# A mixture-of-experts stage of a fused fp32 kernel on one Trainium2 core: units of 32 and of 64 rows by turns in place of units of 64, experts in index order, and the bias rows sent behind the sixth weight piece

## What is computed

```python
def moe_ffn(h, w_router, b_router, w_gate_up, b_gate_up, w_down, b_down):   # h: 512 x 1024
    logits = tok @ w_router + b_router                   # 32 experts
    top_logit, top_idx = lax.top_k(logits, TOP_K)        # TOP_K = 4
    top_w = jax.nn.softmax(top_logit, axis=-1)
    ...
    def expert_block(args):
        xe, e = args
        gu = xe @ w_gate_up[e] + b_gate_up[e]            # 1024 -> 2048
        gate = jnp.minimum(gu[:, :D_FF], SWIGLU_LIMIT)
        up = jnp.clip(gu[:, D_FF:], -SWIGLU_LIMIT, SWIGLU_LIMIT)
        act = (up + 1.0) * gate * jax.nn.sigmoid(SWIGLU_ALPHA * gate)
        return act @ w_down[e] + b_down[e]               # 1024 -> 1024
    ...                                                  # sum over a token's 4 experts, weighted by top_w
```

## Time and profile before

| | |
|---|---|
| median of 3 runs | 3230.87 us (3229.05 to 3233.18) |
| profiled execution, its own time | 3228.85 us |
| its span, first to last instruction | 3227.0 us |
| TensorE busy | 3110.0 us, 96% |
| mean granted clock of TensorE | 0.989 of 2.4 GHz |
| first matmul of the expert loop | 1096.51 us |
| last transposes of the expert stage | 2249.12 us |

### The profile page before, as it was taken

One profiled execution on the slowest core, in us unless ns is written; L12 is line 12 of the kernel. 1 busy time (PEld: TensorE's weight loads), 2 busy tenths in 40 slices (PEclk: granted clock), 3 DMA queues, 4 the chain that ended last, 5 costly groups with the idle time before them and its releaser, 6 DMA issues.

```text
span 3227.0 us, 40980 instructions
## 1 busy us (share of the span) xinstructions
PE 3110.0 (96%) x14106; PEld 1840.9 (57%) x14107; DVE 1303.3 (40%) x2108; ACT 841.3 (26%) x1605; POOL 357.4 (11%) x328
## 2 busy tenths in 40 slices
PE   7999999889999999999999999999999999999999
PEld 5555556464787633333333333333787888888887
DVE  2465564624445312121212121212567577454552
ACT  3354453610211211111111111111325355211100
POOL 0112021431000000000000000000301344000000
PEclk9999999989999899999999999999999999999999
DMA  5324233326312699999999997897411121222121
GB/s 217 118 79 137 91 111 124 121 118 217 122 53 106 233 350 391 374 385 388 389 391 388 379 391 283 310 364 272 155 77 71 59 84 38 94 87 81 63 79 56
DMA packets 190022, 632.85 MB, mean 196 GB/s; under 512 B 18752, under 2 KB 56000, under 8 KB 179168
## 3 DMA queue, kind: packets, MB, share of 16 engines
q1 hardware_dynamic: 161216, 552.79, 44.9%
q0 software_dynamic: 10944, 39.85, 3.5%
q10 hardware_dynamic: 17760, 38.78, 3.4%
HBM read 594.78 MB, written 36.57 MB: 196 GB/s over the span
## 4 chain that ended last, share of the span: by engine, by line
PE 84%; DMA 5%; DVE 4%; issue 2%; ACT 2%; SPq 1%; POOL 1%; ACTq 0%; DVEq 0%; POOLq 0%
PE ps L322 24%; PE ps L2338 17%; PE ps L2312 11%; PE ps L2024 9%; PE ps L271 6%; DMA slot<-in_w_exp 5%; PE ps L2076 2%; PE ps L2567 2%; PE ps L2085 2%; PE ps L1954 1%; PE ps L2539 1%; PE ps L2307 1%; PE ps L2522 1%; PE ps L2303 1%; SPq L1364 1%
## 5 line engine op out<-in xcount | busy, mean ns | idle before, releaser
L2338 PE MATMUL ps<-slot,xT_blk 128*64 128x512 f32 x3200 | 733.9, 599 | 28.2 <-DMA slot<-in_w_exp 25.9
L2338 PEld LDWEIGHTS ps<-slot,xT_blk 128*64 128x64 f32 x3200 | 218.2, 137 | 464.8 <-issue 376.1
L2312 PE MATMUL ps<-slot,aT 128*64 128x512 f32 x1632 | 362.6, 597 | 0.9 <-ACT aT L1715 0.9
L2024 PE MATMUL ps<-hT,slot 128*128 128x512 f32 (+1 forms) x896 | 307.6, 501 | 0.8 <-DVE sum_row L2669 0.8
L2312 PEld LDWEIGHTS ps<-slot,aT 128*64 128x64 f32 x1632 | 117.1, 137 | 238.1 <-issue 238.1
L3063 DVE TENSOR_TENSOR gate<-ps,b_row 128x512 f32<-128x512 f32 x50 | 34.6, 692 | 517.5 <-PE ps L2338 517.2
L2024 PEld LDWEIGHTS ps<-hT,slot 128*128 128x128 f32 x896 | 168.0, 190 | 129.1 <-issue 120.2
L2697 DVE SCALAR_TENSOR_TENSOR conv<-ps,g_conv,conv 128x510 f32<-128x510 f32 (+1 forms) x224 | 133.3, 631 | 179.7 <-ACT conv L1505 176.3
L3059 DVE MEMSET b_there<- 128x1 f32 x50 | 3.0, 59 | 386.7 <-DMA b_few<-in_b_gu 379.3
L1690 ACT ACTIVATE y_row<-ps 128x512 f32<-128x512 f32 x51 | 30.5, 597 | 383.5 <-PE ps L2312 383.5
L322 PE MATMUL ps<-in_t,in_s 128*128 128x264 f32 x528 | 124.7, 386 | 0.5 <-issue 0.5
(11 more groups left out here) (510 smaller groups left out, 4717.7 us busy)
## 6 DMA issues: line engine op xcount, KB each, us to landing
slot<-in_w_exp SPq DMA_DIRECT2D x768, 512.0 KB, 8.5
in_w<-in_w_ffn SPq DMA_DIRECT2D x22, 1024.0 KB, 4.8
expert_rows<-zero SPq DMA_DIRECT2D x4, 4608.0 KB, 22.1
slot<-in_w_xbc SPq DMA_DIRECT2D x8, 2048.0 KB, 7.6
sum_here<-sum_rows ACTq DMA_DIRECT2D x32, 512.0 KB, 3.7
w_modT<-in_w_modT POOLq DMA_DIRECT2D x32, 512.0 KB, 3.8
rnn_w<-in_w_rnn SPq DMA_DIRECT2D x16, 1024.0 KB, 4.8
expert_rows<-y_row ACTq DMA_DIRECT2D x102, 128.0 KB, 5.6
```

What stands on the lines that cost most here:

```text
L2024: last = pe.matmul(ps[:, 2 * (m % 2) + part, 0:n], w[:, (k * 4 + m % 4) * P:(k * 4 + m % 4 + 1) * P], hT[:, k, c0:c0 + n], start=(k == 0), ...
L2312: last = pe.matmul(ps[h * UNIT:(h + 1) * UNIT, 6, :], aT[:, t, d * UNIT:(d + 1) * UNIT], slot[4 + d][:, t * D + h * 512:t * D + (h + 1) * ...
L2338: last = pe.matmul(ps[h * UNIT:(h + 1) * UNIT, 2 * s + t, :], xT_blk[:, k, s * UNIT:(s + 1) * UNIT], slot[i // 4][:, at:at + 512], start=( ...
```

## The change

Turns are kept, but the two units of a turn now have 32 rows (s = 0) and 64 rows (s = 1), and a turn gathers 96 rows. The experts stand in index order. An expert begins where the one before it ended, with either size, and takes units by turns until its tokens have room. With the counts above that makes 60 units in 30 turns. Experts 0, 4, 21, 23 and 30 get a single unit of 32 rows; 1, 11, 22 and 31 a single one of 64; nineteen get one of each (96 rows); expert 9 gets 128 rows, 7 and 24 get 160, and 20 gets 192.

A 32-row matmul takes 32 partitions of output. The two pieces of one K tile are laid out as four quarters of gate and up columns, and the four matmuls go to four column tiles. Down of a 32-row unit is four matmuls of 256 columns for each piece. Gate and up of a unit now come out of the same piece, so the first step on VectorE waits for gu15. `turn_act` moves from behind gu4 to behind gu5, the down pieces from behind gu5 to behind gu7. Buffers that were shared by the two units of a turn (`aT`, `y_row`, `b_row`, `b_few`, the PSUM banks of both) are now one for each size. Every expert gets bias rows for both sizes, eight DMAs in place of four, issued behind piece gu5 in place of gu15. The places come from a scan over the parity of each expert's units.

```diff
-UNIT = 64
-UNITS = SEQ * TOPK // UNIT + NE - 1
+UNIT_ROWS = [32, 64]
+UNIT_AT = [0, 32]
+PERIOD = 96
+TILES = [P // n for n in UNIT_ROWS]
+PART = D // TILES[0]
+PERIODS = -(-(SEQ * TOPK + NE * (UNIT_ROWS[1] - 1)) // PERIOD)
+UNITS = 2 * PERIODS
...
-    TURN_AT, DOWN_AT = 5, 6
+    TURN_AT, DOWN_AT = 6, 8
...
-        for h in range(2):
-            act.dma_start(expert_rows[bass.ds(u * UNIT, UNIT), h * 512:(h + 1) * 512], y_row[h * UNIT:(h + 1) * UNIT, :]).then_inc(s_yrow, 16)
+        rows, first = UNIT_ROWS[s], i * PERIOD + (UNIT_ROWS[1] if s == 0 else 0)
+        width = D // TILES[s]
+        for j in range(TILES[s]):
+            act.dma_start(expert_rows[bass.ds(first, rows), j * width:(j + 1) * width],
+                          y_row[s][j * rows:(j + 1) * rows].rearrange("p t c -> p (t c)")).then_inc(s_yrow[s], 16)
...
-        with sp.Fori(1, NE) as q:
-            u = sp.value_load(first_unit[0:1, bass.ds(q, 1)], min_val=1, max_val=UNITS)
-            e = sp.value_load(expert_at[0:1, bass.ds(q, 1)], min_val=1, max_val=NE - 1)
+        with sp.Fori(1, NE) as e:
+            u = sp.value_load(first_unit[0:1, bass.ds(e, 1)], min_val=1, max_val=UNITS)
             for i in range(GU_PIECES):
                 sp.wait_ge(moe_pe.sem, moe_pe.before(f"gu{i}", u))
                 load_piece(i, e)
-            sp.wait_ge(moe_dve.sem, moe_dve.before("spread", u))
-            load_bias(e)
+                if i == 5:
+                    sp.wait_ge(moe_dve.sem, moe_dve.before("spread", u))
+                    load_bias(e)
...
-        route_dve.after(pe, "rows_before")
-        route_pe.done(pe.matmul(row_of, ones[0:NE, :], rows_before[:].unsqueeze(1).broadcast_to([NE, TT, NE]),
-                                start=False, stop=True, skip_group_check=True), "rows")
-        keep_warm(13, 0)
+        keep_warm(21, 0)
...
+        def down(k, s):
+            quarter, c = divmod(k, 2)
+            half, tile = divmod(quarter, TILES[s])
+            rows, width = UNIT_ROWS[s], D // TILES[s]
+            for j in range(TILES[s]):
+                at = k % 4 * D + j * width
+                last = pe.matmul(ps[j * rows:(j + 1) * rows, Y_BANK_OF[s], 0:width], aT[s][:, 2 * half + c, tile * rows:(tile + 1) * rows],
+                                 slot[4 + k // 4][:, at:at + width], start=(k == 0), stop=(k == DN_PIECES - 1))
...
-                            last = pe.matmul(ps[h * UNIT:(h + 1) * UNIT, 2 * s + t, :], xT_blk[:, k, s * UNIT:(s + 1) * UNIT],
+                            half, tile = divmod(2 * t + h, TILES[s])
+                            rows, first = UNIT_ROWS[s], UNIT_AT[s]
+                            last = pe.matmul(GATE_PS[s][tile * rows:(tile + 1) * rows, half, :], xT_blk[:, k, first:first + rows],
                                              slot[i // 4][:, at:at + 512], start=(k == 0), stop=(k == KD - 1))
...
+        step("filled", dve.tensor_tensor(filled[:].rearrange("p e a b c -> p e (a b c)"), count.unsqueeze(2).broadcast_to([P, NE, 24]),
+                                         capacity.unsqueeze(1).broadcast_to([P, NE, 24]), ALU.is_gt))
+        step("filled_n", dve.tensor_reduce(filled_n[:].rearrange("p e a b -> p (e a b)"),
+                                           filled[:].rearrange("p e a b c -> p (e a b) c"), AX.X, ALU.add))
...
+        step("phase", dve.tensor_tensor_scan(phase[:, 1:NE], phase_step[:, 0:NE - 1], odd_from[:, 0:NE - 1, 0], 0.0, ALU.mult, ALU.add))
...
-                dve.wait_ge(moe_pe.sem, moe_pe.at(f"gu{GU_PIECES - 2}", u))
-                moe_dve.done(dve.tensor_tensor(gate[s][:], ps[:, 2 * s, :], b_row[:, 0, :], ALU.add), "gate")
+                dve.wait_ge(moe_pe.sem, moe_pe.at(f"gu{GU_PIECES - 1}", u))
+                moe_dve.done(dve.tensor_tensor(gate[s][:], GATE_PS[s][:, :, 0:PART], b_row[s][:, :, 0:PART], ALU.add), "gate")
```

More of the change, by code:

```diff
@@ L135 @@
 CST = Columns([("ident", P), ("ones", P), ("le", P), ("gt", P), ("ge", P), ("lt", P),
-               ("expert", NE), ("odd", NE), ("unit", TABLE), ("filled", SEQ // UNIT), ("eps", 1), ("one", 1),
-               ("spot", P), ("pair", PAIR_TABLE + 1), ("token", SEQ // P), ("context", 2)])
+               ("expert", NE), ("filled", 24), ("eps", 1), ("one", 1),
+               ("spot", P), ("period", PERIOD_TABLE + 1), ("token", SEQ // P), ("context", 2)])
 PRM = Columns([("c", 2 * KD), ("b_mod", 2 * N_MOD * KD), ("norm1", KD), ("norm2", KD), ("final", KD),
@@ L899, in program @@
     route_pe = Steps(sem("route_pe"), [f"turned{i}" for i in range(TT)] + ["ranks"]
-                     + [f"turned{i}" for i in range(TT, 2 * TT)] + ["rows", "token", "tables"])
+                     + [f"turned{i}" for i in range(TT, 2 * TT)] + ["token", "tables"])
     TURN_BANKS = [2, 3, 4, 7]
@@ L942, in program @@
     s_few = sem("s_few")
-    s_yrow = sem("s_yrow")
+    s_yrow = [sem(f"s_yrow{s}") for s in range(2)]
+    Y_STORES = [16 * n for n in TILES]
+    GATE_PS = [ps[:, 2:3, :], ps[:, 0:2, :]]
+    AT_BANK, Y_BANK_OF = [3, 5], [7, 6]
     s_all_stored = sem("s_all_stored")
@@ L1673, in _ @@
         moe_xT_act.open(act)
[L1675 removed]
+        for s in range(2):
+            act.sem_inc(s_yrow[s], Y_STORES[s])
         act.wait_ge(s_cleared, 16 * GROUPS)
[L1678 to L1679 removed]
+        route_dve.after(act, "n_periods")
+        n = act.value_load(n_periods[0:1, 0:1], min_val=1, max_val=PERIODS)
         x0_pe.all(act)
@@ L2292, in _ @@
                 c = h * (TT * TOPK // 2) + i
-                last = pe.matmul(ps[:, 0, 0:PAIR_TABLE], at_spot[h][:, i, :], in_pair[:, c, :], start=(c == 0), stop=(c == TT * TOPK - 1))
+                last = pe.matmul(ps[0:PERIOD, 0, 0:PERIOD_TABLE], at_spot[h][:, i, :], in_period[:, c, :], start=(c == 0), stop=(c == TT * TOPK - 1))
         route_pe.done(last, "token")
-        route_dve.after(pe, "expert_in")
-        route_pe.done(pe.matmul(ps[:, 1, 0:TABLE + 2 * NE], ones[0:NE, :], to_table[:], start=True, stop=True), "tables")
+        route_dve.after(pe, "ended")
@@ L2305, in turn_act @@
         def turn_act(s):
-            for t in range(4):
-                last = pe.transpose(ps[:, 5, t * P:(t + 1) * P], gate[s][:, t * P:(t + 1) * P], ident)
-            return last
-        def down(d, t):
-            for h in range(2):
-                last = pe.matmul(ps[h * UNIT:(h + 1) * UNIT, 6, :], aT[:, t, d * UNIT:(d + 1) * UNIT],
-                                 slot[4 + d][:, t * D + h * 512:t * D + (h + 1) * 512],
-                                 start=(d == 0 and t == 0), stop=(d == 1 and t == 3))
+            acts = gate[s][:].rearrange("p t c -> p (t c)")
@@ L2374, in _ @@
         pe.wait_ge(end_act.sem, end_act.at("aT"))
-        pe.wait_ge(moe_act.sem, moe_act.before("y", n * 2))
-        for d in range(2):
-            for t in range(4):
-                pe.wait_ge(exp_loaded[GU_PIECES + 4 * d + t], 16 * NE)
-                last = down(d, t)
+        pe.wait_ge(moe_act.sem, moe_act.before("y", n * 2, 2))
+        for k in range(DN_PIECES):
+            pe.wait_ge(exp_loaded[GU_PIECES + k], 16 * NE)
+            last = down(k, 1)
         end_pe.done(last, "down")
@@ L3442, in _ @@
         w_o.pe.all(pool)
-        pool.memset(b_few[:], 0.0).then_inc(s_few, 1)
+        for s in range(2):
+            pool.memset(b_few[s][:], 0.0).then_inc(s_few, 1)
         route_dve.after(pool, "token_u")
```

258 lines of the change are left out of this document (125 added, 133 removed).

## The result

| | before | changed |
|---|---|---|
| median of 4 runs | 3230.86 us (3229.05 to 3233.18) | 3209.98 us (3209.18 to 3214.02) |
| profiled execution, its own time | 3228.85 us | 3214.02 us |
| span | 3227.0 us | 3212.1 us |
| mean granted clock of TensorE | 0.989 | 0.977 |

The ratio is 0.9937, with a 95% interval of 0.992 to 0.9955: 20.9 us faster. Two further groups of runs of the same two kernels gave 19.6 (3231.16 and 3211.56) and 19.8 (3232.39 and 3212.61).

The account below looks back on a forecast made before the run. TensorE and DMA were both taken to be near their limit, with 41.3 us of waits for pieces. TensorE -59, waits +44 and routing +0.6 summed to -14.4, giving 3216 us, range 3190 to 3242.

Parts of the forecast that it names:

- TensorE's turns: Expert stage: thirty turns of 34.95 us, 1048 in all against 1107 before, a gain of 59 us.
- waits after: Expert stage: TensorE's waits for weight pieces behind light experts come to 85 us, against 41.3 before.
- bias rows: Eight bias DMAs per expert behind gu5: hidden by transfers under way or idle time, cost 0.
- routing: Ahead of the expert stage: longer routing steps, mostly hidden by the filler, cost 0.6 us.
- the stall: Each 32-row slot: TensorE waits 0.75 us ahead of the transposes, as the gate step now needs gu15.
- rival 5: 32-row matmuls: four column tiles don't run together, 0.136 us a record; 3265 us, chance 0.06.
- Changes of width: TensorE's slots: four changes between 32 and 64 columns a turn, 0.15 us each, 0.6 a turn.
- Rival 2: Expert stage: width changes and the new wait on VectorE cost nothing; 3186 to 3200 us, chance 0.13.
- Seven places: Expert stage: waits for pieces stand at experts 2, 5, 12, 22 to 24 and 31, some 85 us.
- the 14 that I had named as a sign of being wrong: Expert stage: the forecast is wrong if a lone light expert costs more than 14 us.
- rival 4: Expert stage: in index order waits take more than TensorE gains, decided at 100 us; 3235 to 3255 us, chance 0.15.
- the books: Expert stage: piece-by-piece model of loads landing 1.28 us apart; gave 43 us of waits before, 85 after.

Follow-up runs that it names:

- short matmuls: Changed kernel with gate, up and down matmuls of 128 columns in place of 512 and 256, all pieces loaded; the stage took 1101.0 us.
- the new units by turns: Changed kernel with its experts stored and routed in the kernel before's alternating light and heavy order; 3249.54 us, ratio 1.0043.
- The packed order: Changed kernel with experts in a fixed order where those of up to 32 rows meet a 32-row unit, 26 turns for 30; 3177.94 us, ratio 0.9831.

## Why the prediction was right, point by point

| term | forecast | measured |
|---|---|---|
| turn before | 44.29 | 44.24 |
| turn after | 34.95 | 34.73 |
| TensorE's turns | -59 | -64.0 |
| waits before | 41.3 | 40.9 |
| waits after | 85 | 89.5 |
| waits, difference | +44 | +48.6 |
| bias rows | 0 | none seen in the waits for pieces, but see below |
| routing | +0.6 | +1.4 in the profiled pair (1096.51 to 1097.92), less than profiles of the changed kernel differ among themselves |
| sum | -14.4 | -15.4 in the stage, -14.8 in the profiled pair, -20.9 in the medians |

*The slots.* The sum of the two was 0.22 too high, 6.6 us in thirty turns. 0.08 of it is the stall (0.67 at 1439.92, where I had 0.75), and the other 0.14 lies within the roundings of the pieces. Four column tiles run together at full pace: the 24 records at 1436.46 are done in 2.78, and 8 of them from 1405.77 with a change of width behind take 1.00, which is 8 x 0.107 + 0.15. At rival 5's 0.136 the 24 would need 3.3. It is out. The Trainium skill ("TensorE: Matmul & The Clock Gate", Measured speedup vs the span model) gives 2.38 for three column tiles. No run here has three, but the efficiency of 0.79 that I took from it doesn't hold for four: a record took 0.107 on four tiles against 0.2135 on two, half in full. *Changes of width.* From 1423.03 eight records of 64 columns take 8 x 0.2135 = 1.71 and down starts at 1424.89, 0.15 later: the value that I took from the transposes. The Trainium skill ("TensorEngine Tiling (Array Packing)", Key Properties) has such changes drain the engine, and this row agrees. Rival 2 had these and the stall at nothing; both were paid.

*The waits.* Seven places, as named. From the distances of `turn_act` starts over 17.47 or 17.26 they come to 12.8 behind experts 0 and 1 (14 forecast), 13.2 behind 4 (11 to 12), 12.4 behind 11 (11), 40.7 around 21 to 23 (40) and 9.0 ahead of 31 (9). Two of the three slots around 21 to 23 lost 14.9 and 15.2, just over the 14 that I had named as a sign of being wrong; the three together have 13.6 each.

The sizes came out better than the reasoning behind them. I had 1.28 us a piece, and with gathers and stores 32.8 an expert. At the lone experts that is right: 32.2 and 32.7. In the experts of 96 rows it is wrong: I let each give back 2 us, with a DMA share under 0.95 among experts 12 to 20. The share between 1500 and 1700 was 1.02, and with short matmuls such an expert costs DMA 34.8, where TensorE's turn is 34.73. So the term that was mis-sized is what an expert of 96 rows costs DMA, by 2 us, and such an expert gives nothing back. If its pieces still took 1.28, what comes with them (gather, stores, bias rows) would be 34.8 - 30.7 = 4.1 a turn in place of my 2.1; that is an estimate, and no run took the gathers, the stores or the doubled bias loads away. The objection stood in rival 4, a stretch at a DMA share of 0.99 with 387 GB/s where 1.28 would be 410. I called that 4% less, and it is 5.6%. I kept the faster pace because it gave the old waits rightly. A pace slower for all pieces wouldn't have been the cure: the books had 114 us of waits at 1.35 a piece and 138 at 1.38, far from 89.5. Books with 1.28 and a dearer turn weren't tried, so how they come within 4.5 us of the trace stays open, and part of it is luck. With the new units by turns they were 18 off (128 against 110).

*The bias rows.* "Cost 0" was right for the pieces as far as the place of the issues goes: TensorE's waits for them sum to 59.5 to 63.0 us in the three profiles of the changed kernel, and to 59.9 and 60.2 with the bias rows at the old place. It missed what the move is worth: with the old place the changed kernel would be 4.4 to 4.9 us slower. The step that failed is that I asked only what the eight issues hold up, and not who waits for the rows. The old kernel never showed it, since there an expert's last piece came well ahead of its use.

*From -15 to -20.* The stage accounts for 15.4. The first pieces take 3.4 less (2.78 for 6.21), and the forecast had no term for them. In the profiled pair most of that was lost again, 1.4 ahead of the first piece and 2.6 behind the stage (977.5 from the last `turn_act` to the end before, 980.1 after), which two of three profiles show and the third (977.8) doesn't. So -14.4 met the pair's -14.8 by luck, at least in part: TensorE gained 5.0 more than forecast, the waits took 4.6 more, and 3.4 that I hadn't counted were lost again in 0.8 more than my 0.6 ahead of the first piece and in 2.6 behind the stage. The medians are 20.9, 19.6 and 19.8 apart, 5 to 6.5 more than forecast. The stage and the first pieces account for 18.8 of that, and the rest is no larger than two executions of one kernel differ.

*Rival 4* asked the right question. Index order does cost 44.6 us on the old units, and 100 us of waits would have been passed with one or two lone units more: the same kernel by turns had 128 and was slower. That the result is on the fast side hangs on the token counts of this input.

## What to carry to other kernels

When a stage is close to two limits, price each with the other one taken away (an eighth of each transfer, a quarter of each matmul), and expect an edit to give at most the distance to the nearer line: here 64 us of TensorE work bought 15 in the stage, and 22 us more bought 2. Then look at the share along the stage too: a line that is an average (35.5) can hide that one kind of expert costs 32 and another 35. Two parts of an edit can each lose and together win, when one removes the slack on which the other one's order depends; so test them in all four combinations before judging either. And for a small transfer that is moved, ask who waits for it where its engine runs on the heels of the data, not only what its issue delays.

The packed order is the fastest version that ran, 3177.94, 1.7% below before. It was fixed for this input's token counts; choosing the order on the chip from the counts, as the kernel before did with two classes, was not tried.

## What was unexpected in the hardware

TensorE's clock falls in the waits and comes back late, and at the place shown here it cost next to nothing. Behind the wait of 10.70 at 1953.12, 24 records of 64 columns took 8.07, 0.336 each, against 0.2135 at 2.4 GHz. Stretches of the changed kernel around the waits and one without any:

```profile
1940.00:1960.00 20.00, 9.30 (x44) 2.65 (x38) 2.20 (x6) 1.70 (x2) 0.00 (x0) 0.66 1.03 410
1960.00:1980.00 20.00, 18.73 (x152) 6.85 (x152) 5.03 (x12) 4.63 (x12) 1.27 (x2) 1.00 1.03 409
1700.00:1720.00 20.00, 20.00 (x158) 7.09 (x156) 3.53 (x9) 3.69 (x8) 0.18 (x1) 1.00 1.01 394
```

The 0.66 is a mean of the two levels. In steps of 2 us the granted clock was 0.50, which is 1.2 GHz, from 1946 to 1958, and 1.00 from 1960 on: it fell while TensorE stood still and stayed down for some 5 us of matmuls. At that level a piece took 1.71 us (four records at 0.427), slower than pieces arrive. But the pieces behind it were late anyway:

```profile
1962.02 1.08 PE L2361 MATMUL ps<-slot,xT_blk 128*64 128x512 f32 x4 [0.47 <-DMA slot<-in_w_exp]
1963.30 1.08 PE L2361 MATMUL ps<-slot,xT_blk 128*64 128x512 f32 x4 [0.20 <-DMA slot<-in_w_exp]
```

Some 4 us after the last slow record TensorE, back at full clock, waits for DMA again, so by then it had made good what the lower clock cost. With short matmuls the granted clock was 0.68 in the mean over the whole stage, and the stage took 1101.0, where the packed order took 1097.9 at 0.94. Both suggest that the clock isn't what makes the waits dear; no run held it up during a wait to show it.
